# U rows of 24 instead of 16 first keys in dense blocks, in an order that follows the rankings, and two rankings of the second token tile placed sooner

## The reference, cut to what matters

```python
q = (h @ w_query)                                  # 8 heads, two halves of 128
s = einsum('bshcd,hckd->bshck', q, sub_keys)       # 128 scores per half
top_s, top_i = top_k(s, 16)                        # per half
cand = top_s[..., 0, :, None] + top_s[..., 1, None, :]
best_s, best_i = top_k(cand, 16)                   # 16 of 256
eid = i1 * 128 + i2                                # first key * 128 + second key
g = softmax(best_s)
a = gelu(einsum('td,thkd->thk', h, expert_u[eid])) # one dot of 2048 for each pick
out = einsum('thk,thkd->td', g * a, expert_v[eid]) # weighted sum of V rows
```

## Time and profile before

| | |
|---|---|
| median of 3 runs | 1729.92 us (1729.15 to 1730.08) |
| profiled execution, its own time | 1728.9 us |
| its span | 1727.2 us |
| PE busy | 1462.0 us, 85% |
| DVE busy | 1377.8 us, 80% |
| POOL busy | 790.3 us, 46% |
| ACT busy | 689.9 us, 40% |
| DMA | 596.32 MB, mean 345 GB/s |
| granted TensorE clock, mean | 0.928 |

### The profile page before, as it was taken

One profiled execution on the slowest core, in us unless ns is written; L12 is line 12 of the kernel. 1 busy time (PEld: TensorE's weight loads), 2 busy tenths in 40 slices (PEclk: granted clock), 3 DMA queues, 4 the chain that ended last, 5 costly groups with the idle time before them and its releaser, 6 DMA issues.

```text
span 1727.2 us, 22269 instructions
## 1 busy us (share of the span) xinstructions
PE 1462.0 (85%) x8242; PEld 1171.4 (68%) x8242; DVE 1377.8 (80%) x2543; ACT 689.9 (40%) x995; POOL 790.3 (46%) x592
## 2 busy tenths in 40 slices
PE   9999999999979987878775555577768779999996
PEld 8988999988668877767774454476667744444442
DVE  6666656666797997875787899999978998788888
ACT  5665456564201144554564455455547610100000
POOL 3210000000233344654557565767656458687862
PEclk9999999999989999998998878888888769999998
DMA  9886443467689899999999999999999899999996
GB/s 323 284 264 220 122 147 117 131 199 263 243 326 397 316 381 425 395 422 422 380 400 422 424 415 408 413 424 422 424 411 411 348 409 400 403 402 410 417 400 268
DMA packets 161710, 596.32 MB, mean 345 GB/s; under 512 B 25592, under 2 KB 78932, under 8 KB 101380
## 3 DMA queue, kind: packets, MB, share of 16 engines
q0 software_dynamic: 79232, 449.12, 64.7%
q1 hardware_dynamic: 82368, 145.77, 23.3%
HBM read 700.19 MB, written 2.10 MB: 407 GB/s over the span
## 4 chain that ended last, share of the span: by engine, by line
DVE 30%; PE 27%; DMA 24%; issue 8%; POOL 7%; DVEq 2%; ACT 2%; POOLq 0%; SPq 0%; ACTq 0%
DMA u_slot<-in_expert_u_dram,eid 14%; PE psum_all L658 14%; DMA v_slot<-in_expert_v_dram,eid 9%; DVE u_slot L1968 9%; DVE u_slot L1966 9%; POOL v_slot L616 6%; PE psum_all L798 4%; DVE xh L2046 3%; PE psum_all L823 1%; PE psum_all L1107 1%; PE psum_all L779 1%; POOL u_slot L593 1%; ACT v_slot L1434 1%; PE psum_all L685 1%; DVE xh L2054 1%
## 5 line engine op out<-in xcount | busy, mean ns | idle before, releaser
L593 POOL DMA_INDIRECT u_slot<-in_expert_u_dram,eid x256 | 319.7, 1249 | 436.4 <-DVE u_slot L1968 283.1
L1107 PE MATMUL psum_all<-ident,v_slot 128*128 128x128 f32 x2304 | 348.6, 316 | 191.3 <-ACT v_slot L1434 186.6
L616 POOL DMA_INDIRECT v_slot<-in_expert_v_dram,eid x256 | 433.4, 1693 | 157.6 <-issue 73.1
L1107 PEld LDWEIGHTS psum_all<-ident,v_slot 128*128 128x128 f32 x2304 | 313.9, 165 | 218.7 <-ACT v_slot L1434 208.7
L1434 ACT ACTIVATE v_slot<-v_slot,gate 128x2048 f32<-128x2048 f32 x144 | 287.6, 2001 | 260.0 <-DMA v_slot<-in_expert_v_dram,eid 246.4
L1966 DVE SCALAR_TENSOR_TENSOR u_slot<-u_slot,xh 128x1024 f32<-128x1024 f32 x256 | 312.6, 1221 | 92.1 <-DMA u_slot<-in_expert_u_dram,eid 75.5
L1968 DVE SCALAR_TENSOR_TENSOR u_slot<-u_slot,xh 128x1024 f32<-128x1024 f32 x256 | 312.7, 1222 | 0.0
L2046 DVE SCALAR_TENSOR_TENSOR xh<-v_slot,gate,xh 128x2048 f32<-128x2048 f32 x100 | 235.2, 2352 | 46.3 <-DMA v_slot<-in_expert_v_dram,eid 39.0
L1583 DVE TENSOR_TENSOR w_lo<-w_ring,w_hi 128x512 fp32r<-128x512 f32 x240 | 156.8, 688 | 79.1 <-ACT w_hi L1161 75.9
L658 PE MATMUL psum_all<-act_hi,w_hi 128*128 128x256 f32 x640 | 184.7, 289 | 1.3 <-DVE w_lo L1583 1.2
L658 PE MATMUL psum_all<-act_hi,w_lo 128*128 128x256 f32 x640 | 180.7, 282 | 0.0
(11 more groups left out here) (320 smaller groups left out, 1858.9 us busy)
## 6 DMA issues: line engine op xcount, KB each, us to landing
w_ring<-in_w_in_dram SPq DMA_DIRECT2D x88, 512.0 KB, 4.7
u_slot<-in_expert_v_dram SPq DMA_DIRECT2D x40, 1024.0 KB, 8.8
wo_ring<-in_w_out_dram SPq DMA_DIRECT2D x32, 512.0 KB, 5.2
wq_ring<-in_w_query_dram SPq DMA_DIRECT2D x32, 512.0 KB, 7.8
x_slot<-in_expert_u_dram SPq DMA_DIRECT2D x16, 1024.0 KB
w_ring<-in_cmp_k_w_dram POOLq DMA_DIRECT2D x16, 512.0 KB, 5.7
w_ring<-in_cmp_v_w_dram POOLq DMA_DIRECT2D x16, 512.0 KB, 4.1
u_slot<-in_expert_u_dram,eid POOLq DMA_INDIRECT x256
```

Source lines behind the costliest of these rows:

```text
L593: nc.gpsimd.indirect_dma_start(out=u_slot[slot][:, :], out_offset=None, in_=expert_u[0], in_offset=bass.IndirectOffsetOnAxis(ap=eid[:, n, ...
L616: nc.gpsimd.indirect_dma_start(out=v_slot[slot][:, :], out_offset=None, in_=expert_v[0], in_offset=src, bounds_check=bound - 1, oob_is_err ...
L1107: ins = nc.tensor.matmul(bank[(4 if n < PH else 0) + c // 4][:, P * (c % 4):P * (c % 4) + P], v_slot[v_ring(m)[0]][:, P * c:P * c + P], id ...
```

## The change

- FU = 24 keys have their U in blocks. SP loads 24 blocks instead of 16; PE and ACT take 32 more steps (up to V pick 72) and ACT 8 more `u_gelu`. The gathers of U, and those of V in units 14 and 15, skip the last 24 first keys instead of the last 16, and `gates_of` and `late_weights` use the new bound.
- The 8 new keys are the numbers F_LATE = 32 to 39, whose results lie over `scores`, in the order 32, 33, 36, 37, 34, 35, 38, 39 (`x_place`). Before the results of the first of them, ACT waits for ranking 7 (`ids_ok` 9), before the fifth for ranking 9, before the seventh for ranking 11.
- The units of tile 1 take the heads in the order 0, 6, 1, 7, 2, 3, 4, 5 (`unit_head`), so that rankings 8 to 11 read the scores of heads 0, 6, 1 and 7.
- Ranking 10 moves from (8,9) to (8,5), ranking 11 from (9,1) to (8,9). The others stay.
- The U ring has 6 slots up to pick 174 instead of 126. V's ring stays; its widening and the first weigh wait for 24 blocks.
- `dense_out` copies 16 of 40 keys instead of 24; `weigh` gets a second multiply for keys 32 to 39, 64 elements.

```diff
@@ -32,7 +32,7 @@
...
-U_WIDE = 126
+U_WIDE = 174
...
@@ -48,14 +48,16 @@
...
 FG = FD - FX
+FU = 24
+F_LATE = FD - (FU - FX)
 ROWS = (NKEY - FD) * NKEY
-ROWS_X = (NKEY - FX) * NKEY
+ROWS_X = (NKEY - FU) * NKEY
...
-IDS_AT = {(0, 4): 1, (8, 9): 10, (9, 1): 11, (9, 9): 12, (10, 1): 13, (10, 9): 14, (11, 1): 15}
+IDS_AT = {(0, 4): 1, (8, 5): 10, (8, 9): 11, (9, 9): 12, (10, 1): 13, (10, 9): 14, (11, 1): 15}
 IDS_AT.update({(n, 1): n + 1 for n in range(1, 9)})
 UNIT_AT = {(64 * (n - 3) + 4) // 5 + 4: n for n in range(4, 13)}
...
 
 def key_of(f):
     return NKEY - FX + f if f < FX else NKEY - FD + f - FX
...
+def x_place(i):
+    return i if i < FX else F_LATE + (0, 1, 4, 5, 2, 3, 6, 7)[i - FX]
...
+def unit_head(n):
+    t, h = divmod(n, PH)
+    return t, (h, (0, 6, 1, 7, 2, 3, 4, 5)[h])[t]
...
 
...
-            first = NKEY * key_of(i)
+            first = NKEY * key_of(x_place(i))
...
-        for i in range(RX, FX):
+        for i in range(RX, FU):
             sp.wait_ge(S["ut_mm"], 4 * (i - RX + 1))
             load_x_block(i)
         for f in range(FD):
...
             if m == U_WIDE:
-                pool.wait_ge(S["ut_mm"], 4 * FX)
+                pool.wait_ge(S["ut_mm"], 4 * FU)
             if RU_X <= m < U_WIDE:
                 pool.wait_ge(S["dots_done"], dots_value(m - RU_X + 1))
             elif m >= U_WIDE + RU - RU_X:
...
             if m == V_WIDE:
-                pool.wait_ge(S["xs_mm"], FX)
+                pool.wait_ge(S["xs_mm"], FU)
             if RV_X <= m < V_WIDE:
                 pool.wait_ge(S["v_used"], m - RV_X + 1)
             elif V_WIDE + RV - RV_X <= m < PE_PICKS + RV:
...
             j = X_FIRST + m
-            if j < 4 * FX:
+            if j < 4 * FU:
...
@@ -1108,7 +1119,7 @@
...
+            if j <= 4 * FU:
                 u_dots(j - 1)
...
             act.wait_ge(S["dense_mm"], g + 1)
...
-            nc.scalar.activation((dense0[:, FX:FD, cols], dense1g[:, :, cols])[t], src[:, FX:FD, :], ACT.Copy
+            nc.scalar.activation((dense0[:, FX:F_LATE, cols], dense1g[:, 0:F_LATE - FX, cols])[t], src[:, FX:F_LATE, :], ACT.Copy
                                  ).then_inc(S["dense_ok"], 1)
...
         def u_gelu(i):
...
-            nc.scalar.activation(dense0[:, i, :], bank[2][:, 0:P], ACT.Gelu_apprx_tanh)
-            nc.scalar.activation(dense1x[:, i, :], bank[2][:, P:SEQ], ACT.Gelu_apprx_tanh).then_inc(S["xa_ok"], 1)
+            f = x_place(i)
+            if i == FX:
+                act.wait_ge(S["ids_ok"], 9)
+            if i == FX + 4:
+                act.wait_ge(S["ids_ok"], 11)
+            if i == FX + 6:
+                act.wait_ge(S["ids_ok"], 13)
+            dst = dense1x[:, i, :] if i < FX else dense1g[:, f - FX, :]
+            nc.scalar.activation(dense0[:, f, :], bank[2][:, 0:P], ACT.Gelu_apprx_tanh)
+            nc.scalar.activation(dst, bank[2][:, P:SEQ], ACT.Gelu_apprx_tanh).then_inc(S["xa_ok"], 1)
...
         def u_step(j):
 
-            if j < 4 * FX:
+            if j < 4 * FU:
                 u_out(j)
-            if j > 4 and j % 4 == 1 and j <= 4 * FX + 1:
+            if j > 4 and j % 4 == 1 and j <= 4 * FU + 1:
                 u_gelu(j // 4 - 1)
...
 
         def ids(n):
 
-            t, h = divmod(n, PH)
+            t, h = unit_head(n)
...
-                V.scalar_tensor_tensor(b_val[:, n, :], b_id[:, 0, n, :], float(NKEY - FX), w_late[:, i, :], ALU.is_ge, ALU.mult)
+                V.scalar_tensor_tensor(b_val[:, n, :], b_id[:, 0, n, :], float(NKEY - FU), w_late[:, i, :], ALU.is_ge, ALU.mult)
...
-            V.tensor_scalar(kept[:, :], b_id[:, 0, n, :], float(NKEY - FX), -1.0, ALU.is_lt, ALU.mult)
...
-                V.scalar_tensor_tensor(wide[:, :], b_id[:, 0, n, :], float(NKEY - FX), b_val[:, n, :], ALU.is_ge, ALU.mult)
...
@@ -2032,10 +2051,12 @@
...
             if g == 0:
-                dve.wait_ge(S["xa_ok"], FX)
+                dve.wait_ge(S["xa_ok"], FU)
             dve.wait_ge(S["dense_ok"], g + 1)
...
+            late = (dense0[:, F_LATE:FD, G_TOK * b:G_TOK * b + G_TOK], dense1g[:, F_LATE - FX:FG, G_TOK * b:G_TOK * b + G_TOK])[t]
+            V.tensor_tensor(late, src[:, F_LATE:FD, :], late, ALU.mult)
             V.tensor_tensor(cols, src[:, 0:FX, :], cols, ALU.mult).then_inc(S["weigh_ok"], 1)
...
```

More of the change, by code:

```diff
@@ L1110, in _ @@
             ins.then_inc(S["v_used"], 1)
-            if j <= 4 * FX:
+            if j <= 4 * FU:
                 u_dots(j - 1)
@@ L1990, in gates_of @@
                 V.reciprocal(g_inv[:, n:n + 1], g_sum[:, n:n + 1])
-            V.tensor_scalar(kept[:, :], b_id[:, 0, n, :], float(NKEY - FX), -1.0, ALU.is_lt, ALU.mult)
+            V.tensor_scalar(kept[:, :], b_id[:, 0, n, :], float(NKEY - FU), -1.0, ALU.is_lt, ALU.mult)
             dve.wait_ge(S["gelu_ok"], n + 1)
@@ L1997, in gates_of @@
                 V.tensor_tensor(gate[:, n, :], u_dot[:, n, :], b_val[:, n, :], ALU.mult)
-                V.scalar_tensor_tensor(wide[:, :], b_id[:, 0, n, :], float(NKEY - FX), b_val[:, n, :], ALU.is_ge, ALU.mult)
+                V.scalar_tensor_tensor(wide[:, :], b_id[:, 0, n, :], float(NKEY - FU), b_val[:, n, :], ALU.is_ge, ALU.mult)
                 dve.drain()
```

## The result

The changed kernel takes 1737.23 us (median), the kernel before 1730.68 us in the same comparison: ratio 1.0030, interval 1.0018 to 1.0042, so 5.2 us slower by the ratio (the medians lie 6.6 us apart). Ratios compare only executions in the chip's faster state; differences in us go by the medians where no ratio is named. The forecast was 1727.8 us, 2.1 us faster. The profiled execution took 1734.73 us with a span of 1733.0, against 1728.9 and 1727.2.

A forecast was written before the change was run, and what follows sets the result against it. DMA was taken as the bound from 631 to about 1056 us, then DMA and DVE together, DVE alone in the last 75 us. The terms sum to -2.1 us, giving 1727.8 us, range 1715 to 1741.

The forecast's parts named there:

- Part 1: U gathers fetch 8 rows fewer each: -1.2 us before 631 us, -9.4 to 877, -7.4 to 1056, -10 to 1405.
- The sign that I named: DVE's wait for U rows in the stretch 631 to 877 us would fall by about 8 us.
- Part 2: Eight more x blocks, all between 877 and 1056 us: +20.3 us; the extra PE and ACT steps cost nothing.
- Part 3: Six U slots for 48 gathers longer, and rankings closer together: +3 us, bounds 0 and +9.
- The cluster of rankings: Three rankings at dots 129, 133 and 137 drain the DMA queue; those after the first lose up to 3 us each.
- Part 4: One more DVE instruction in each of 32 weighs, +4.9 us; a wait for ACT's smaller copy shortens, -1.5 us.
- The one wait for ACT's copy: DVE's wait of 4.7 us for ACT's copy may shorten: -1.5 us, bounds 0 and -4.7.
- Part 5: The tail: the last 32 V gathers lose 8 rows each, -0.8 us; the rest moves with the last weigh.
- A: Bytes count to the end, DVE has more slack than its waits show, weighs vanish: -12 us, 1718; chance 0.22.
- B: Rankings clustered on six slots push DMA share under about 0.95, dots 129 to 174: +10.4 us, 1740; chance 0.15.
- C: A block's fixed transfer part is not shared: eight blocks cost +17 us more, +15 in all, 1745; chance 0.04.
- D: An ACT wait is not met in time, so POOL stands: up to 18 us, 1746; chance 0.04.

## Why the prediction was wrong, point by point

- **Part 1, right in its sum.** -28.0 us, and 25 measured as a difference in the changed kernel; the 3.4 us that the rows gave between units 7 and 10, for 7.4, and the 13.8 behind unit 10, for 10, offset each other. The sign that I named failed as worded: DVE's wait for U rows in the first stretch went from 45.1 to 51.4 us. But all its idle time there fell from 58.4 to 51.8, and the stretch is 7 us shorter.
- **Part 2, about right in size, in part in place.** The stretch with the blocks lasts 13 us longer, forecast 15.9; DVE's wait there is 30.1 us, forecast 30. With blocks and all U rows that stretch is only 16.4 us longer than before, where Parts 2 and 3 had 23.3; the rest is paid around it. What the eight blocks cost by themselves: the run with blocks and all U rows is 1.81% above before; less the order (0.31%) and the weighs (about 1 us) that leaves 25 us for blocks and six slots together, where Parts 2 and 3 had 23.3. How they share these is open: 16 us for the blocks if the slots cost their 9 us here, nearer 24 if they are covered, for which the 0.7 us of the run with U_WIDE 150 speak weakly.
- **Part 3, wrong in its parts.** The cluster of rankings costs nothing. The six slots by themselves cost 9 us in the kernel before, and the nearest row, one dip of share, could not price that. What they cost in the changed kernel stays open; if it is little, the +3 was near by luck.
- **Part 4, too high or hidden in part.** The instruction was sized rightly (216 ns against 0.22 us), but 3.1 us of 4.9 reach the last weigh, and none at the end is clear of noise. The one wait for ACT's copy fell from 4.7 to 3.5 us, 1.2 of the 1.5 us.
- **Part 5, the step that failed.** The prediction let the tail change by -0.8 us and for the rest move "as a block with the last weigh"; it grew by 6.2. I read `unit_head` as a change of when rankings run and priced it only by its waits on ACT. It also changed which V rows lie in the tail and which DMA engine has to bring them, a term that the prediction does not have; the order alone, with no other part of the change, lengthened the tail by 8.9 us and cost 0.31%. The prediction also counted on V rows being in time behind 1650 us, which held: the loss lies ahead of that. Taking the measured 6.2 for -0.8 gives -2.1 + 7.0 = +4.9, and 5.2 was measured.
- **The rivals.** A fell: DVE was near its bound, and the last two stretches gave 6 us, not 13.7. B forecast the sign, not the place: the last weigh was not late, and between the rankings (933 to 1000 us) the DMA share stayed at 0.98 to 1.01; it was 0.95 once, from 1031 to 1062 us. C fell: blocks and six slots together cost 25 us, where unshared fixed parts would have added 17 to the 23.3. The fit in the Trainium skill (DMA: Bandwidth & Descriptors, Anatomy of one DMA — SWDGE (gpsimd) path) gives each transfer 2.0 us beside its bytes; it is stated for transfers that POOL issues, and the runs do not show such a part for SP's blocks behind one another. D fell: no wait of ACT in the blocks' stretch is longer than 4.6 us. The side on which it came out had a chance of 0.25.

## What to carry to other kernels

Where a gather skips rows, count the rows of the fullest DMA engine (eight partitions each), stretch by stretch, before you price bytes: an edit that only permutes work permutes these counts too, and the counts depend on the data. Read GB/s beside the DMA share: from 1550 to 1650 us the share stayed at 0.99 to 1.01 while the rate was 391 and 413 GB/s instead of 407 and 422. And test a permutation apart from the saving that needs it: here another permutation takes the loss away, 1729.05 us.

## What the runs showed of the hardware that I had not expected

- Skipping 32 rows of 128 in each of 40 gathers saved 23 us of 99 when the rows were spread and nothing when they were all the rows of four engines or half those of eight.
- The same bytes in the same time read as a share of 0.76 or 0.84, by how the load was spread (four engines idle, or eight at half load).
- Two U slots less for 48 gathers cost 9 us, for the first 24 of them 1 us, at a DMA share that read 0.99 over the 60 us where the rate began to fall, and 0.97 in the last 20 of them.
